# The second block's two attentions in pairs of heads, probabilities normalised before their transposes, values as the stationary operand

## The reference

```python
proj = rmsnorm(h_res) @ w_in          # q_lat, kv_lat, k_pe, g_mla, na_q, na_k, na_v, g_na
# MLA: 8 heads, 128 + 64 features of q and k, values of 128, all 272 keys
s = einsum('bqhd,bkhd->bhqk', q_nope, k_nope) + einsum('bqhr,bkr->bhqk', q_pe, k_pe)
y_mla = einsum('bhqk,bkhd->bqhd', softmax(s * scale), v) * silu(g_mla)
# NA: 16 heads of 64; 4 grid rows of 64 columns; a query sees a window of 16 columns in all
# rows, with a bias by distance, and the 16 meta keys, with a bias per head and key
s = concat([q @ k_win * scale + bias, q @ k_meta * scale + meta_bias])
y_na = (softmax(s) @ [v_win, v_meta]) * silu(g_na)
out = h_res + concat([y_mla, y_na]) @ w_out       # the 256 real tokens
```

## Time and profile before

| | us |
|---|---|
| median of three runs | 1320.96 (1319.97 to 1323.59) |
| profiled execution: span of its instructions | 1319.6 |
| of it, TensorE busy | 1287.5 |
| MLA attention | 42.42 |
| NA projections, queries and keys (1088.91 to 1144) | 55.09 |
| NA attention, to the last value product | 111.71 |
| from there to the first final product | 2.32 |
| final products and stores | 25.97 |

### The profile page before, as it was taken

One profiled execution on the slowest core, in us unless ns is written; L12 is line 12 of the kernel. 1 busy time (PEld: TensorE's weight loads), 2 busy tenths in 40 slices (PEclk: granted clock), 3 DMA queues, 4 the chain that ended last, 5 costly groups with the idle time before them and its releaser, 6 DMA issues.

```text
span 1319.6 us, 27677 instructions
## 1 busy us (share of the span) xinstructions
PE 1287.5 (98%) x10106; PEld 1220.6 (93%) x10106; DVE 844.0 (64%) x1478; ACT 662.2 (50%) x1153; POOL 127.6 (10%) x149
## 2 busy tenths in 40 slices
PE   6999999999999999999999999999889999999998
PEld 6999999999999999999999999999878769978778
DVE  6676656777667547666558676676566645456565
ACT  5554544555555445445436464554456556434443
POOL 3000000440000000000003510000110000002210
PEclk9999999999999999999999999999989999999999
DMA  7555744345556536557444465566433204433332
GB/s 278 191 188 192 230 153 156 126 144 193 184 188 226 189 103 202 191 186 239 163 133 139 136 195 182 189 212 212 133 109 128 97 1 134 138 132 96 110 99 65
DMA packets 55689, 209.87 MB, mean 159 GB/s; under 512 B 6417, under 2 KB 8465, under 8 KB 55489
## 3 DMA queue, kind: packets, MB, share of 16 engines
q1 hardware_dynamic: 54048, 203.45, 47.0%
q0 software_dynamic: 1424, 5.42, 1.4%
q10 hardware_dynamic: 144, 0.06, 0.0%
HBM read 207.86 MB, written 1.05 MB: 158 GB/s over the span
## 4 chain that ended last, share of the span: by engine, by line
PE 93%; DVE 4%; issue 1%; ACT 1%; DMA 0%; DVEq 0%; ACTq 0%; SPq 0%
PE bank L1043 26%; PE bank L1044 26%; PE bank L1045 25%; PE bank L1081 2%; PE bank L1390 2%; DVE w_lo L654 1%; PE bank L1355 1%; DVE h_lo L673 1%; PE bank L1344 1%; PE bank L1353 1%; PE bank L1354 1%; PE bank L1281 1%; PE bank L1386 1%; PE bank L1283 1%; PE bank L1282 1%
## 5 line engine op out<-in xcount | busy, mean ns | idle before, releaser
L1043 PE MATMUL bank<-h_hi,w_hi 128*128 128x256 f32 (+1 forms) x1992 | 568.6, 285 | 17.6 <-DVE w_lo L654 11.8
L1044 PE MATMUL bank<-h_lo,w_hi 128*128 128x256 f32 (+1 forms) x1992 | 564.4, 283 | 0.0
L1045 PE MATMUL bank<-h_hi,w_lo 128*128 128x256 f32 (+1 forms) x1992 | 559.5, 281 | 0.0
L654 DVE TENSOR_TENSOR w_lo<-w_raw,w_hi 128x1024 fp32r<-128x1024 f32 (+1 forms) x360 | 465.5, 1295 | 81.1 <-ACT w_hi L388 79.7
L388 ACT ACTIVATE w_hi<-w_raw 128x1024 fp32r<-128x1024 f32 (+1 forms) x360 | 397.3, 1107 | 92.7 <-PE bank L1045 69.7
L1043 PEld LDWEIGHTS bank<-h_hi,w_hi 128*128 128x128 f32 x1992 | 377.7, 190 | 30.5 <-issue 26.0
L1044 PEld LDWEIGHTS bank<-h_lo,w_hi 128*128 128x128 f32 x1992 | 376.9, 189 | 0.8
L1045 PEld LDWEIGHTS bank<-h_hi,w_lo 128*128 128x128 f32 x1992 | 377.4, 189 | 0.0
L1043 PE MATMUL bank<-g_hi,w_hi 128*128 128x256 f32 x832 | 232.7, 280 | 0.4 <-DVE x_res L839 0.3
L1044 PE MATMUL bank<-g_lo,w_hi 128*128 128x256 f32 x832 | 232.3, 279 | 0.0
L1045 PE MATMUL bank<-g_hi,w_lo 128*128 128x256 f32 x832 | 232.2, 279 | 0.0
(11 more groups left out here) (169 smaller groups left out, 1318.0 us busy)
## 6 DMA issues: line engine op xcount, KB each, us to landing
w_raw<-in_w SPq DMA_DIRECT2D x296, 512.0 KB, 3.3
w_raw<-in_wd SPq DMA_DIRECT2D x64, 704.0 KB, 4.1
rel_bias<-in_relbias POOLq DMA_DIRECT2D x16, 192.0 KB, 2.7
btab_sb<-in_btab POOLq DMA_DIRECT2D x1, 1536.0 KB, 9.9
x_res<-in_xT SPq DMA_DIRECT2D x2, 512.0 KB, 5.1
out_T<-x_res SPq DMA_DIRECT2D x8, 128.0 KB, 1.7
rope_sb<-in_rope POOLq DMA_DIRECT2D x1, 272.0 KB, 3.9
mats_sb<-in_mats POOLq DMA_DIRECT2D x1, 192.0 KB, 3.9
```

What stands on the lines that cost most here:

```text
L654: dve.tensor_tensor(wlo[:, slot, 0:cols], raw[:, slot, 0:cols], whi[:, slot, 0:cols].bitcast(F32), ALU.subtract).then_inc(lo_ready[slot], 1)
L1043: pe.matmul(o, h, xh, start=first, stop=False)
L1044: pe.matmul(o, h, xl, start=False, stop=False)
L1045: return pe.matmul(o, lo, xh, start=False, stop=last)
```

## The change

A unit becomes a member of a step: two heads (hh = 0 and 1) on one row tile, 8 steps for MLA and 16 for NA. The scores of both heads stand in two banks; their 64-row products lie on the two halves of the array's rows. The softmax scales go into the norms' gains once, ahead of the second block. In NA one fused VectorE instruction adds bias and score of a unit, negates, and takes the minimum, which is the negative of the maximum; GpSimd prepares a whole 272-column bias tile for each unit in one of four buffers, with a load of four grid rows. VectorE divides the probabilities by their sum before TensorE transposes them. The third key block is keys 144 to 271, with the rows of V that the second block has already counted set to zero, so all blocks are 128 high. V is stationary and the transposed probabilities move, so the result lies feature-major at once: for MLA 128 features of one head, for NA two heads on the two halves of the output partitions. `O32` of the second block, its transposes and the pads go; the gate product, high and low part of each tile run inside the attention loops. A fill is no longer halved. The final outputs use banks 0 to 3.

```diff
-        S = sb("scores_sb", [P, 2, 3 * BLK])
-        Pr = sb("probs", [P, 2, 3 * BLK])
-        PT = sb("probs_T", [P, 2, 3 * BLK])
-        O32 = sb("attn_out", [P, 2, D])
+        s_all = sb("scores_sb", [P, 4 * TM])
+        pr_all = sb("probs", [P, 4 * TM])
+        PT = sb("probs_T", [P, 4, 3 * BLK])
+        S, Pr = (a[:, 0:6 * BLK].rearrange("p (s c) -> p s c", s=2) for a in (s_all, pr_all))
+        S4, Pr4 = (a[:].rearrange("p (s c) -> p s c", s=4) for a in (s_all, pr_all))
         sml = sb("small_sb", [P, SMALL])
...
+            rel = sb("rel_bias", [P, 4, TM], F32, second)
+
+        QL0 = 2 * TM
+        KEYS = (0, BLK, TM - BLK)
         latw = {"kv": (0, TM), "ql": (QL0, T)}
...
             pool.wait_ge(fx_done, KT)
-            pool.memset(yhi[:, 2 * TM:QL0].bitcast(F32), 0.0).then_inc(pad_set, 1)
-            pool.memset(ylo[:, 2 * TM:QL0].bitcast(F32), 0.0).then_inc(pad_set, 1)
-            for h in range(NH):
-                if h >= 2:
-                    pool.wait_ge(s_add, LAYERS * HEADS + 2 * (2 * (h - 1)) + PRIME)
-                pool.dma_start(rel[:, h % 2], relbias[h]).then_inc(rel_loaded[h % 2], 16)
-                pool.wait_ge(rel_loaded[h % 2], 16 * (h // 2 + 1))
-                if h == 0:
-                    pool.wait_ge(c_loaded, C_LOADS)
-                pool.tensor_tensor(rel[:, h % 2], rel[:, h % 2],
-                                   cmask[:].unsqueeze(1).broadcast_to([P, 6, GW]), ALU.add).then_inc(rel_ready, 1)
+            pool.wait_ge(c_loaded, C_LOADS)
+            for i in range(2 * NH):
+                h, t = 2 * (i // 4) + i % 2, i // 2 % 2
+                if i >= 4:
+                    pool.wait_ge(nm_done, U0 + 2 * MH + i - 3)
+                pool.dma_start(rel[:, i % 4, 0:T], relbias[h][:, 2 - 2 * t:6 - 2 * t, :].rearrange("p r c -> p (r c)"))\
+                    .then_inc(rel_loaded[i % 4], 16)
+                pool.tensor_copy(rel[:, i % 4, T:TM], metab[:, h, :])
+                pool.wait_ge(rel_loaded[i % 4], 16 * (i // 4 + 1))
+                r4 = rel[:, i % 4, 0:T].rearrange("p (r c) -> p r c", r=4)
...
+            def probs_T(v0, step):
+
+                for hh in range(2):
+                    v = unit(v0, step, hh)
+                    act.wait_ge(tr_done, U0 + v + 1)
+                    act.activation(PT[:, v % 4], bank[4 + hh][:, 0:3 * BLK], ACT.Copy).then_inc(pt_done, 1)
...
+            def attention(v0, steps, mla):
+                for i in range(steps + 3):
+                    if i < steps:
+                        for hh in range(2):
+                            v = unit(v0, i, hh)
+                            act.wait_ge(nm_done, U0 + v + 1)
+                            src = score_bank(i, hh, True) if mla else S4[:, v % 4]
+                            act.activation(Pr4[:, v % 4], src, ACT.Exp, bias=nm[:, v % 32:v % 32 + 1],
+                                           scale=1.0 if mla else -1.0, accum_out=sums[:, v % 32:v % 32 + 1])\
+                               .then_inc(exp_done, 1)
+                    if mla and i < steps:
+                        gate_tanh(i, sgate[:, i])
+                    if 1 <= i <= steps:
+                        probs_T(v0, i - 1)
+                    if not mla and i < FILL:
+                        split2(FILL0 + i + LEAD)
+                    if not mla and i < 8:
+                        act.wait_ge(w_used[(FILL0 + i) % SLOTS], uses2(FILL0 + i))
+                        gate_tanh(8 + i, fill_out(i))
+                    p = (i - 3) // 2
+                    if i >= 3 and i % 2:
+                        for y in (2 * p, 2 * p + 1) if mla else (8 + p,):
+                            y_high(y)
...
+            for kind, factor in (("qn", MLA_SCALE), ("qpe", MLA_SCALE), ("naq", HD ** -0.5)):
+                gain = G_HEAD + HEAD_GAIN[kind]
+                dve.tensor_scalar(sml[:, gain:gain + 1], sml[:, gain:gain + 1], factor, None, ALU.mult)
+            dve.reduce_sum(vmask[:], ident[:, P - META:P], AX_X).then_inc(second_set, 1)
             norm(7, TM)
+            dve.wait_ge(second_set, 1)
 
...
 
-            def y_product(y, b):
-                dve.wait_ge(ot_done, LAYERS * QT + y + 1)
...
-                dve.scalar_tensor_tensor(out=y32(y), in0=b[:, 0:T], scalar=0.5, in1=sgate[:, y % 8],
+            def y_product(y, o):
+
+                if y >= 2:
+                    dve.wait_ge(y_lo, y - 1)
+                dve.scalar_tensor_tensor(out=g32[:, y % 2], in0=o, scalar=0.5, in1=sgate[:, y % 8],
                                          op0=ALU.mult, op1=ALU.mult).then_inc(y_done, 1)
 
             def y_low(y):
...
-                            dve.tensor_copy(V[0:np_, tt, c * 512:(c + 1) * 512], bank[out_bank(outs, i)][0:np_, :])\
-                               .then_inc(pj_taken, 1)
+                            v_out, v_in = V[:, tt, c * 512:(c + 1) * 512], bank[out_bank(outs, i)][:]
+                            if tt < 2:
+                                dve.tensor_copy(v_out, v_in).then_inc(pj_taken, 1)
+                            else:
+                                dve.tensor_scalar(v_out, v_in, vmask[:], None, ALU.mult).then_inc(pj_taken, 1)
...
+            def neg_max(v0, step, mla):
+
+                for hh in range(2):
+                    v = unit(v0, step, hh)
+                    c, scores = v % 32, score_bank(step, hh, mla)
+                    dve.wait_ge(sc_done, U0 + v + 1)
+                    if mla:
+                        dve.tensor_reduce(nm[:, c:c + 1], scores, AX_X, ALU.max, negate=True).then_inc(nm_done, 1)
+                    else:
+                        i = v - v0
+                        dve.wait_ge(rel_ready, i + 1)
+                        dve.tensor_tensor_reduce(S4[:, v % 4], scores, rel[:, i % 4], -1.0, 3.0e38, ALU.add, ALU.min,
+                                                 nm[:, c:c + 1]).then_inc(nm_done, 1)
+
+            def normalise(v0, step):
+
+                v = unit(v0, step, 0)
+                c = v % 32
+                dve.wait_ge(exp_done, U0 + v + 2)
+                dve.reciprocal(rec[:, c:c + 2], sums[:, c:c + 2]).then_inc(rec_done, 1)
+                dve.wait_ge(rec_done, STEPS0 + v // 2 + 1)
+                for hh in range(2):
+                    pr = Pr4[:, (v + hh) % 4]
+                    dve.tensor_scalar(pr, pr, rec[:, c + hh:c + hh + 1], None, ALU.mult).then_inc(pn_done, 1)
+
...
+                for i in range(steps + 3):
+                    if 1 <= i <= steps:
+                        normalise(v0, i - 1)
+                    if i < steps:
+                        neg_max(v0, i, mla)
+                    if mla and i < steps:
+                        silu(i, i, sgate[:, i], silu_all)
+                    if not mla and i < FILL:
+                        split2(FILL0 + i + LEAD)
+                    m = i - 1
+                    if not mla and 0 <= m < 8:
+                        silu(8 + m, m, fill_out(m), fill_taken)
+                    elif not mla and 8 <= m < FILL:
+                        piece, o = FILL0 + m, m - 8
+                        dve.wait_ge(w_used[piece % SLOTS], uses2(piece))
+                        dve.tensor_tensor(x[:, o, 0:T], fill_out(m), x[:, o, 0:T], ALU.add).then_inc(fill_taken, 1)
+                    if i >= 4 and i % 2 == 0:
+                        p = (i - 4) // 2
+                        for y in (2 * p, 2 * p + 1) if mla else (8 + p,):
+                            y_low(y)
+                    if i >= 3 and i % 2:
+                        p = (i - 3) // 2
+                            dve.wait_ge(pv_done, U0 + unit(v0, i - 2, 1) + 1)
+                            for hh in range(2):
+                                y_product(2 * p + hh, bank[6 + p % 2][:, hh * T:(hh + 1) * T])
+                            dve.wait_ge(pv_done, U0 + unit(v0, i - 2, 1) + 1)
+                            y_product(8 + p, bank[2 + p % 2][:, 0:T])
...
+            def scores(v0, step, mla):
+
+                p, tok = step // 2, slice(step % 2 * P, (step % 2 + 1) * P)
+                for hh in range(2):
+                    v, o = unit(v0, step, hh), score_bank(step, hh, mla)
+                    if mla:
+                        if step >= 2:
+                            pe.wait_ge(exp_done, U0 + v - 3)
+                        pe.matmul(o, qn[:, 2 * p + hh, tok], kn[:, 2 * p + hh, :], start=True, stop=False)
+                    else:
+                        if step >= 1:
+                            pe.wait_ge(nm_done, U0 + v - 1)
+                        r = slice(hh * HD, (hh + 1) * HD)
+                        pe.matmul(o, qn[r, p, tok], kn[r, p, :], start=True, stop=True).then_inc(sc_done, 1)
+                for hh in range(2) if mla else ():
+                    r, o = slice(hh * MR, (hh + 1) * MR), score_bank(step, hh, True)
+                    pe.matmul(o, qp[r, p, tok], kp[r, :], start=False, stop=True).then_inc(sc_done, 1)
+
+            def transposes(v0, step):
+
```

(93 more changed lines are left out.)

186 lines of the change are left out of this document (21 added, 165 removed).

## The result

The changed kernel is slower: 1331.01 us in the median of 4 runs (1330.1 to 1332.1) against 1321.83 of the kernel before (4 runs, 1319.97 to 1323.59). The ratio is 1.0073, with a 95% interval of 1.006 to 1.0087. Forecast were 1304 us and a ratio of 0.987. The profiled execution has a span of 1330.3 us, 10.7 more than before.

The account below looks back on a forecast made before the run. TensorE, busy 98% of the span, was taken to bound the kernel. MLA 7.1, projections 1.8, NA and end 8.1 make 17.0 us off the profiled 1319.6: 1302.6, as a median 1304 us; range 1297 to 1314.

Parts of the forecast that it names:

- NA, TensorE: TensorE's work per step of the NA attention: 6.47 us against 7.0 before, setting the end of the values at 106.8 us.
- the ScalarE and VectorE loop: In NA, the loop from exponentials through copies, splits and normalising takes 6.0 us a step, only just under TensorE's 6.47.
- The clock: In NA, the prediction fails also if TensorE's waits lower the granted clock; beside long waits it had been 0.73.
- MLA: First attention of the second block: steps of 4.21 us, stage 35.2 us against 42.4, of which 7.1 us saved is taken.
- the second costs 0.46 if they queue: MLA scores: the second 64-row product of a step is taken to queue at 0.46 us, making the scores 2.03 us.
- Projections: Between the attentions: eight pairs of output transposes leave, 0.22 us each, 1.8 us saved.
- NA, values and scores: TensorE's products in an NA step: scores 1.11 us, twelve value passes plus one border 1.52 us.
- rival A: MLA and NA: products on the array's halves run side by side, TensorE's NA step 5.69 us, total 1300 us; chance 0.25.
- rival C: In NA, VectorE's fused maximum costs 1.02 us instead of 0.44, loop 7.1 us, total 1314 us; chance 0.07.
- GpSimd: In NA, preparing biases takes u = 3.4 us a unit, 6.8 a step, bounds 3.2 and 3.75; it binds from 3.47.
- Rivals B and D: NA: B, VectorE delays GpSimd, 1312 us, chance 0.11; D, GpSimd's load-then-add chain with slowest loads, 1326 us, chance 0.05.
- The end: Final products and stores: four interleaved pairs of transposes leave, the last stage falls from 23.36 to 22.4 us, 1.0 saved.

Follow-up runs that it names:

- The bank taken first: In the changed kernel, VectorE's SiLU or residual of the previous fill moves ahead of its weight split: 1293.7 us, ratio 0.9793.
- products in the wait: In the changed kernel, 22 products that nobody reads are issued ahead of each fill from the fifth on: 1319.4 us, ratio 0.9992.
- bank first, biases ahead: In the changed kernel, VectorE's SiLU or residual precedes its weight split, and GpSimd's next load and copy precede its add: 1289.4 us, ratio 0.9756.
- The fastest kernel: Changed kernel with VectorE freeing the bank before splitting, ScalarE splitting before copies, GpSimd's next load before its add, some final products before the last values: 1276.5 us.
- biases ahead: In the changed kernel, GpSimd issues the next unit's load and copy before this unit's add: 1330.2 us, ratio 1.0071.
- ScalarE's split moved alone: In the changed kernel, ScalarE splits the next weights ahead of its two copies of the transposes, VectorE's order stays: 1318.0 us, ratio 0.9976.
- ScalarE first and biases ahead: In the changed kernel, ScalarE's weight split goes ahead of its two transpose copies and GpSimd's next load and copy ahead of its add: 1279.0 us.

## Why the prediction was wrong

**The step that failed** is "NA, TensorE", 6.47 us a step with the conclusion "so TensorE sets it", together with the sentence of the ScalarE and VectorE loop that "it fits under 6.47". Both loops were reckoned each for itself. The wait of a fill for `fill_taken` is in neither, though it ties them: VectorE's SiLU stood in the 6.0 us loop as 0.34 us of work, and not as the thing that TensorE's next fill waits for. Followed round, the ring is 0.81 + 0.49 + 0.35 + 0.48 + 0.95 + 1.23 + 0.34 + handovers and 2.95 of fill, 7.8 us. With the prediction's own durations it is 1.52 + 0.48 + 0.80 + 0.97 + 1.14 + 0.34 + 3.03 = 8.3 us, so it could have been worked out from the rows of before. It is an unlisted rival, at 13 x (7.8 - 6.47) = 17 us for the waits, which alone cancels the forecast gain of 17.0. The bank taken first shows it (37.3 us back). In the sum of the 15 distances the forecast had 4.14 + 4.95 + 13 x 6.47 = 93.2 us, and 124.0 were measured. With the mean of 7.87 us from the kernel with products in the wait, the 30.8 us between them are some 18 for the ring and 14 for the clock, less 1 in the first two steps.

**The clock** stood in the last paragraph as a danger, without a price. It cost 12.0 us in the eleven distances in which the products in the wait keep it up, and some 14 in all thirteen by the estimate above.

**MLA**: forecast a stage of 35.2, measured 32.33, steps of 3.77 in place of 4.21. The step that was mis-sized is the second 64-row product, "the second costs 0.46 if they queue"; it cost nothing (scores 1.58 in place of 2.03, 0.45 us less a step). The 128-row scores' 0.92 and the values' 1.53 were right.

**Projections**: 1.8 forecast, 1.45 measured.

**NA, values and scores**: 1.52 forecast for twelve values, 0.81 measured; scores 1.11, measured 0.66. TensorE's own step is 5.30 and not 6.47: rival A was right in its mechanism and even undersized it (5.69), and its 1300 us would still have been beaten by the ring. The Trainium skill, "TensorEngine Tiling (Array Packing)", "Key Properties", states that different tiles work in parallel; the trace agrees, 0.66 us for four passes against 0.65 for two.

**ScalarE and VectorE**: 6.0 reckoned, 5.95 measured where nothing else binds (bank first, biases ahead). The fused instruction is 0.44 us long as taken, so rival C is out. The fastest kernel shows that this loop isn't fixed: in another order it is under 5.3.

**GpSimd**: u = 3.4 was taken. With the bank first it is 3.0 to 3.2 in the steady steps with the add at 0.73, so at or under the lower bound of 3.2; it still held the steps there at 6.0 to 6.3, where the loop behind it allows 5.95, because TensorE was faster than reckoned. The chain that ended last runs there through its loads (2.3 us) and adds alone:

```profile
1219.27 0.73 POOL L390 TENSOR_TENSOR rel_bias<-rel_bias,colmask_sb 128x256 f32<-128x256 f32 x1 [1.22 <-DMA rel_bias<-in_relbias]
...
1222.31 0.74 POOL L390 TENSOR_TENSOR rel_bias<-rel_bias,colmask_sb 128x256 f32<-128x256 f32 x1 [1.60 <-DMA rel_bias<-in_relbias]
```

Rivals B and D, no cause of the result (biases ahead: 1330.2), appear with ScalarE's split moved alone. What the prediction set against the change is seen the other way round for certain: a normalising instruction that starts behind one of GpSimd takes longer. In the changed kernel six of 32 took 0.52 to 0.87 us instead of 0.36. Here, GpSimd and then VectorE, the two of a step take 1.14 us instead of 0.63:

```profile
1193.71 0.74 POOL L390 TENSOR_TENSOR rel_bias<-rel_bias,colmask_sb 128x256 f32<-128x256 f32 x1 [0.69 <-DMA rel_bias<-in_relbias]
```

```profile
1193.74 1.14 DVE L1002 TENSOR_SCALAR probs<-probs,reciprocals 128x272 f32<-128x272 f32 x2
```

**The end**: forecast 1.0 off the final products, measured none; their clock is 0.94, where it was 1.00 before. In the kernel with ScalarE first and biases ahead they run at 1.00 and take 24.6 us from the first of them to the end, 1.35 less than before, so the term was right and the clock hid it.

## What to carry to other kernels

When a pipeline is made coarser, follow each buffer that an engine waits for round the whole ring, through every instruction that stands ahead of its release in the other engines' orders, and compare the ring with the busiest engine; sums per engine don't show it. Where a ring binds, look for the link where an instruction with slack (here a weight split for later) stands ahead of the release: moving that one is free. Give a wait on TensorE a second price, that of the clock behind it, and time two ways of opening the ring, for each uncovers another next bound.

## What the runs showed of the hardware

- With waits of 2.6 to 3.0 us once in a step, the granted clock fell in eight of the thirteen steps that had them (0.21 us between products for 0.117). With 22 products more in the wait it stayed at 1.00. Where no wait was over 1.2 us, in the kernel with ScalarE first, no stretch of the steps was under 1.00.
- 64-row passes on alternating row halves overlap wholly: 0.66 us for four, 0.65 for two on one half. Twelve 64-column values alternating between column halves take 0.81 us, against 1.07 in order of heads; how much of either is overlap is open.
- VectorE's split (two inputs in SBUF) and GpSimd hinder each other, and the later one pays. GpSimd's add took 1.75 us for 0.72 and its copy of 16 columns 1.16 for 0.21 behind a split. VectorE's normalising (one input) behind an add took 0.87 for 0.36. The split behind an add took 1.60 for 1.23, as here in the kernel with bank first and biases ahead, GpSimd and then VectorE:

```profile
1233.37 0.73 POOL L395 TENSOR_TENSOR rel_bias<-rel_bias,colmask_sb 128x256 f32<-128x256 f32 x1 [0.22 <-DMA rel_bias<-in_relbias]
```

```profile
1233.58 1.60 DVE L672 TENSOR_TENSOR w_lo<-w_raw,w_hi 128x1024 fp32r<-128x1024 f32 x1 [2.19 <-ACT w_hi L406]
```
